# Order of PSUM reads and weight-chunk splits on VectorE and ScalarE in a two-layer hybrid attention trunk

## The reference

```
h = rms_norm(x); z = h @ w_in                 # columns cq, ckv, kr, gq, gk, gv, a, g
# A, latent attention: q = rms(cq) @ w_uq, k and v = rms(ckv) @ w_ukv, norms, rope,
#    8 heads, block-causal softmax(q k^T) v
# B, gated linear attention, 4 heads, chunks of 64 tokens:
#    la = log_sigmoid(z_a @ w_gate + b)/16; suffix sums and decays = exp(...)
#    state = state * decay + (k * exp(..))^T v;  o = q @ state;  rms_norm(o) * silu(z_g)
x = x + concat(rms(A), B) @ w_out
h = rms_norm(x); u = causal_dwconv(h @ w_up); x = x + (silu(gate) * up) @ w_down
```

## Time and the profile before

| | |
|---|---|
| median of 3 runs | 2252.37 us (2251.55 to 2254.59) |
| the profiled execution, its own time | 2252.84 us |
| its span, first to last instruction | 2251.1 us |
| TensorE busy | 2171.3 us (96%) |
| VectorE busy | 1511.8 us (67%) |
| ScalarE busy | 1006.6 us (45%) |
| mean granted TensorE clock | 0.989 |

### The profile page before, as it was taken

The page is one execution under the profiler, slowest core; times in us unless marked ns, Lnnn a source line. Parts: engine busy times, 40 slices in busy tenths (PEclk is TensorE's granted clock), DMA queues, the critical chain, the costliest instruction groups (busy, mean ns, idle before and its releaser), DMA issues. The chain is left out here.

```text
span 2251.1 us, 26696 instructions
## 1 busy us (share of the span) xinstructions
PE 2171.3 (96%) x11132; PEld 1834.0 (81%) x11132; DVE 1511.8 (67%) x1804; ACT 1006.6 (45%) x1151; POOL 15.9 (1%) x18
## 2 busy tenths in 40 slices
PE   7799889999999999999997998899999999999999
PEld 6687768888888888888885876688888888888887
DVE  5554455787777777777754554568777777787676
ACT  5555544444334344444454554354344334444442
POOL 0010000000000000000000100000000000000000
PEclk9999999999999999999998999999999999999999
DMA  7544335565555555555553444355655555555553
GB/s 214 177 137 135 131 112 187 170 204 172 189 191 192 194 187 186 189 189 190 192 173 117 156 142 140 114 188 169 206 187 176 190 191 191 189 189 184 194 190 139
DMA packets 293708, 391.90 MB, mean 174 GB/s; under 512 B 10944, under 2 KB 200180, under 8 KB 293588
## 3 DMA queue, kind: packets, MB, share of 16 engines
q1 hardware_dynamic: 293332, 390.00, 52.4%
q0 software_dynamic: 256, 0.20, 0.1%
HBM read 388.07 MB, written 2.10 MB: 173 GB/s over the span
## 5 line engine op out<-in xcount | busy, mean ns | idle before, releaser
L828 DVE TENSOR_TENSOR lo<-raw,hi 128x2048 fp32r<-128x2048 f32 (+2 forms) x372 | 841.2, 2262 | 416.0 <-ACT hi L514 414.6
L514 ACT ACTIVATE hi<-raw 128x2048 fp32r<-128x2048 f32 (+2 forms) x372 | 704.0, 1893 | 657.8 <-PE G L1309 351.4
L1366 PE MATMUL G<-hx,hi 128*128 128x512 f32 x1408 | 497.4, 398 | 0.0
L1366 PE MATMUL X<-hx,hi 128*128 128x512 f32 x1408 | 496.7, 397 | 0.0
L1367 PE MATMUL X<-hx,lo 128*128 128x256 f32 x1408 | 395.2, 281 | 0.0
L1367 PE MATMUL G<-hx,lo 128*128 128x256 f32 x1408 | 395.2, 281 | 0.0
L1366 PEld LDWEIGHTS X<-hx,hi 128*128 128x128 f32 x1408 | 264.3, 188 | 64.6
L1366 PEld LDWEIGHTS G<-hx,hi 128*128 128x128 f32 x1408 | 264.4, 188 | 64.3
L1367 PEld LDWEIGHTS G<-hx,lo 128*128 128x128 f32 x1408 | 266.0, 189 | 0.8
L1367 PEld LDWEIGHTS X<-hx,lo 128*128 128x128 f32 x1408 | 266.0, 189 | 0.0
L1307 PE MATMUL G<-hi,hx 128*128 128x512 f32 (+1 forms) x512 | 203.0, 397 | 15.7 <-DVE gv L1098 11.0
(11 more groups left out here) (250 smaller groups left out, 2230.1 us busy)
## 6 DMA issues: line engine op xcount, KB each, us to landing
raw<-in_w_up SPq DMA_DIRECT2D x176, 1024.0 KB, 5.1
raw<-in_w_down SPq DMA_DIRECT2D x88, 1024.0 KB, 5.0
raw<-in_w_in SPq DMA_DIRECT2D x56, 1024.0 KB, 5.1
raw<-in_w_out SPq DMA_DIRECT2D x32, 1024.0 KB, 5.0
raw<-in_w_uq SPq DMA_DIRECT2D x8, 768.0 KB, 4.7
raw<-in_w_in SPq DMA_DIRECT2D x8, 640.0 KB, 4.1
raw<-in_w_ukv SPq DMA_DIRECT2D x4, 1024.0 KB, 5.1
xk<-in_x SPq DMA_DIRECT2D x4, 512.0 KB, 10.9
```

What stands on the lines that cost most here:

```text
L514: act.activation(hi[:, k % SLOTS, 0:n], raw[:, k % SLOTS, 0:n], ACT.Copy).then_inc(hi_ready, 1)
L828: dve.tensor_tensor(lo[:, s, 0:n], raw[:, s, 0:n], hi[:, s, 0:n].bitcast(F32), ALU.subtract).then_inc(lo_ready, 1)
L1366: pe.matmul(bank, w_hi[:, at:at + P], hx[:, tile, :], start=tile == 0, stop=False)
```

## The change

The change alters no operation, no count and no shape. It moves operations against the splits in the lists of ScalarE and VectorE, alike in both layers; the lists of TensorE, GpSimd and SyncE stay as they are. VectorE: gk's `by_token` and `copy_kraw(0)` go from behind splits 14 and 15 to ahead of split 14, `copy_kraw(1)` ahead of split 15, the `la` step ahead of 16, gq's `by_token` ahead of 20, each `q_out` ahead of the next split, `copy_values` of odd heads ahead of splits 30, 32, 34 and 36, all `a_split` ahead of split 37, states 0 and 1 ahead of 39, `copy_o(0)` ahead of 40, states 2 and 3 ahead of 41, `gate_o(0)` and `copy_o(1)` ahead of 43, `gate_o(1)` ahead of 44. ScalarE: `copy_v(0)` ahead of split 15, `copy_v(1)` ahead of 16, the decays ahead of `k_square(1)`, `exps` ahead of `a_square`, `a_split` ahead of split 37 and of `silu(0)`, `o_square(0)` ahead of 41; `q_square(0)` and `q_square(1)` each go behind one more split.

```diff
 ScalarE
                 act.activation(la, la, ACT.Exp, scale=-1.0).then_inc(gate_soft.sem, 1)
+                copy_v(0)
                 split(l, 15)
                 act.activation(la, la, ACT.Ln, bias=ones[:, 0:1]).then_inc(gate_soft.sem, 1)
-                copy_v(0)
+                copy_v(1)
                 split(l, 16)
-                copy_v(1)
                 k_square(0)
                 split(l, 17)
-                k_square(1)
                 act.activation(la, X[:, 2:4, :], ACT.Exp, scale=1.0 / TAU).then_inc(gate_decay.sem, 1)
                 act.activation(decay, X[:, 0, 0:16], ACT.Exp, scale=1.0 / TAU).then_inc(gate_decay.sem, 1)
+                k_square(1)
                 split(l, 18)
...
+                split(l, 23)
                 q_square(0)
-                split(l, 23)
-                q_square(1)
...
                 split(l, 24)
+                q_square(1)
...
                     split(l, k + 2)
+                    exps(2 * p)
+                    exps(2 * p + 1)
                     if p >= 1:
                         a_square(2 * p - 1)
-                    exps(2 * p)
-                    exps(2 * p + 1)
...
                 a_square(HEADS - 1)
-                silu(0)
-                split(l, 37)
                 for h in range(HEADS):   # a_split, high part
...
+                split(l, 37)
+                silu(0)
                 split(l, 38)
...
                 silu(1)
+                o_square(0)
                 split(l, 41)
-                o_square(0)
 VectorE
-                split(l, 14)
                 by_token(U_GK, K_GK + 3, gk)
+                copy_kraw(0)
+                split(l, 14)
+                copy_kraw(1)
                 split(l, 15)
-                copy_kraw(0)
-                split(l, 16)
-                copy_kraw(1)
                 dve.scalar_tensor_tensor(la, X[:, 2:4, :], 0.0, la, ALU.min, ALU.subtract).then_inc(gate_log.sem, 1)
+                split(l, 16)
                 split(l, 17)
...
-                split(l, 20)
                 by_token(U_GQ, K_GQ + 3, gq, GDK ** -0.5)
+                split(l, 20)
+                q_out(0)
                 split(l, 21)
-                q_out(0)
                 q_rope(0)
+                q_out(1)
                 split(l, 22)
-                q_out(1)
                 q_rope(1)
+                q_out(2)
                 split(l, 23)
-                q_out(2)
+                q_out(3)
                 q_rope(2)
                 split(l, 24)
-                q_out(3)
                 q_rope(3)
...
-                    split(l, k + 2)
                     if p >= 1:
                         copy_values(2 * p - 1)
+                    split(l, k + 2)
...
+                copy_values(HEADS - 1)
                 split(l, 36)
-                copy_values(HEADS - 1)
-                split(l, 37)
                 for h in range(HEADS):   # a_split, low part
-                    if h == 6:
-                        split(l, 38)
...
+                split(l, 37)
+                split(l, 38)
...
-                split(l, 39)
                 state_step(0)
                 state_step(1)
+                split(l, 39)
+                copy_o(0)
                 split(l, 40)
-                copy_o(0)
+                state_step(2)
+                state_step(3)
                 split(l, 41)
                 add_to_x_when_done(l, U_OUT, a_rs)
                 split(l, 42)
-                state_step(2)
-                state_step(3)
                 gate_o(0)
+                copy_o(1)
                 split(l, 43)
                 add_to_x_when_done(l, U_OUT + 1, a_rs)
-                copy_o(1)
+                gate_o(1)
                 split(l, 44)
-                gate_o(1)
```

More of the change, by code:

```diff
@@ L652, in _, with copy_v @@
                 act.activation(la, la, ACT.Exp, scale=-1.0).then_inc(gate_soft.sem, 1)
+                def copy_v(j):
+                    act.wait_ge(slot_free, done(l, K_UKV + j))
+                    act.activation(v[:, :, 512 * j:512 * j + 512], bank2(U_UKV + 2 * j + 1), ACT.Copy).then_inc(v_copied.sem, 1)
+                copy_v(0)
                 split(l, 15)
@@ L655, in _ @@
                 act.activation(la, la, ACT.Ln, bias=ones[:, 0:1]).then_inc(gate_soft.sem, 1)
-                def copy_v(j):
-                    act.wait_ge(slot_free, done(l, K_UKV + j))
-                    act.activation(v[:, :, 512 * j:512 * j + 512], bank2(U_UKV + 2 * j + 1), ACT.Copy).then_inc(v_copied.sem, 1)
                 def k_square(j):
@@ L1090, in by_token @@
                     ins.then_inc(unit_free.sem, 1)
-                split(l, 14)
-                by_token(U_GK, K_GK + 3, gk)
                 def copy_kraw(j):
@@ L1098, in copy_kraw @@
                     dve.tensor_copy(kraw[:, :, 512 * j:512 * j + 512], bank2(U_UKV + 2 * j)).then_inc(unit_free.sem, 1)
+                by_token(U_GK, K_GK + 3, gk)
+                copy_kraw(0)
+                split(l, 14)
+                copy_kraw(1)
                 split(l, 15)
-                copy_kraw(0)
-                split(l, 16)
-                copy_kraw(1)
                 dve.wait_ge(gate_soft.sem, gate_soft.at(l, 3))
                 dve.scalar_tensor_tensor(la, X[:, 2:4, :], 0.0, la, ALU.min, ALU.subtract).then_inc(gate_log.sem, 1)
+                split(l, 16)
                 split(l, 17)
```

## The result

The changed kernel takes 2166.03 us (median of 4 runs, 2165.29 to 2166.48), against 2253.48 us for the kernel before beside it (4 runs, 2251.55 to 2254.91). The ratio is 0.9616, with a 95% interval of 0.9604 to 0.9627: 3.8% faster. Predicted were 2167 us in a range of 2161 to 2187.

The account below looks back on a forecast made before the run. TensorE was taken to bound the kernel. Waits 64.0, clock 17.9 and overlap 4.5 us sum to 86.4 us, taking 2252.84 us to 2166.4; the forecast was 2167 us, range 2161 to 2187.

Parts of the forecast that it names:

- What bounds the kernel: Whole kernel: TensorE, busy 2171.3 of 2251.1 us, sets the end; only its idle time, clock and matmul overlap count.
- The ten lines: TensorE's waits at steps the change moves, in both layers: 28 waits, 64.0 us in all.
- Step 1: TensorE's waits: walking the new order with old durations, none of the ten lines' waits is left, 64.0 us saved.
- four narrow places: Time in hand in the walk: copy_v(0) 1.6 us, copy_kraw(1) 1.4, q_out(2) 2.3, gate_o(1) 2.1.
- Steps 2 and 3: TensorE: full clock returns behind long waits, 17.9 us; matmul overlap lost at 28 waits returns, 4.5 us.
- Step 4: ScalarE's own moves (k_square(1), q_square, silu(0)) cost nothing; at most 1 us a layer if keys come late.
- Step 5: SyncE's loads, issued later behind a late lo, cost nothing; bounds 0 and 1 us for each late load.
- A: Rival: the narrow places come back as short waits, about 2 us at each of eight, 2183 us; chance 0.12.
- B: Rival: TensorE's idle time goes but the clock stays as it was, 2184 us; chance 0.04.
- C: Rival: loads become the bound, ten a layer each late by 1 us, 2187 us; chance 0.03.
- E: Rival: nothing changes, since the waits have another last releaser than the one named, 2252 us; chance 0.01.
- D: Rival: VectorE's reads ahead of subtractions make lo late and TensorE wait for it, slower, 2314 us; chance 0.02.

Follow-up runs that it names:

- e6: Changed kernel plus two reductions of constants on VectorE between the wait for the second key half and its copy, copy_kraw(1): 2165.90 us.
- e7: Changed kernel plus six reductions of constants on VectorE between the wait for the second key half and its copy, copy_kraw(1): 2171.70 us.
- three stage kernels: Kernel before with the new order in one stretch only: split 14 to the attention loop 2209.64 us, attention loop 2240.35, from split 37 on 2219.60.
- e4: Kernel before with the new order only in the attention loop, up to split 36, on both engines: 2240.35 us, ratio 0.9954.
- e5: Kernel before with the new order only from split 37 on, on both engines: 2219.60 us, ratio 0.9859.
- e11: Kernel before with VectorE's new list, and on ScalarE only copy_v(0) moved ahead of split 15 and the Ln: 2165.07 us, ratio 0.9613.
- e2: Kernel before with the new order on ScalarE alone, VectorE as before: 2243.07 us, ratio 0.9953.
- e9: Changed kernel plus ten reductions on VectorE between copy_kraw(0) and the subtraction of chunk 14: 2173.21 us.

## Why the prediction was right

Point by point, by its own steps. **What bounds the kernel**: the reading held. The ten lines were the whole of what could be had, and VectorE and ScalarE, with 30% and more of idle time, did not become the bound. **Step 1, idle time**: 64.0 us forecast, 63.9 measured. The walk through the new order with the old durations gave the margins to 0.1 us at all four narrow places, and e6 and e7 bracket the narrowest. The wide ones hold as well: `a_split` ends 8.0 us before it is wanted (1305.56 against 1313.59; the walk 8), the first two states 4.9 us (1319.03 against 1323.94; the walk 5), the others 7.6 us (1337.84 against 1345.48; the walk 7). That the waits are each their own is shown by the three stage kernels. **Steps 2 and 3, clock and overlap**: 17.9 + 4.5 = 22.4 us forecast, 23.2 measured as the fall in busy time. The sum held because every long wait went, and with them every stretch at a lower granted clock; for a part of the change the same reading was off by 4 us, as e4 and e5 show. Had the change removed only some of the waits, a forecast as near as this one would have been luck. **Step 4, ScalarE's other moves at nothing**: right for the whole change (e11), but for a reason that the step did not give: `q_square`'s move frees `q_out(2)` by itself (e2), and VectorE's move frees it again. The gain could be had twice and is counted once. **Step 5, loads**: ScalarE waits for loads of `w_in` three times, 4.5 us in all, as it did before the change (three times, 4.6 us), and e9, with the load of chunk 17 some 6 us later still, has no more (4.2 us).

**The rivals.** A did not come: the narrow places held in both layers. B fell: the clock is 1.00 over the mixer. C and E fell with the waits. D, the slower case, is a real mechanism, and its price was half right. VectorE does go in order, and a late subtraction does reach TensorE (e9), but through the next PSUM read in VectorE's list rather than through `lo`. The step that was mis-sized is "4.1 us late stands against a further 4.8 us before TensorE asks": what was in hand is 3.4 us, because I took TensorE's next wish for chunk 14 and not the copy that VectorE must do between. The 7.3 us in that step is also added up wrongly: it leaves out the 4.1 us by which the walk's `lo` is late already, so by its own numbers it is 4.1 + 4.8 + 2.5 = 11.4 us, and with the measured 3.4 it is 10.0. Neither slip mattered for the result.

## What to carry to other kernels

When an engine that does not set the end is idle a third of the time and the engine that does still waits for it, look at what stands ahead of the awaited operation in its list: here each was prefetch work, two chunks ahead of need, which was itself waiting. Put reads that free a bank ahead of prefetch, and then walk the new order through with measured durations, following every list to the next operation that TensorE asks for and not only to the delayed one. Price the clock behind waits as a whole, since of two waits of the same length and place one can cost it and the other not.

## What the runs showed of the hardware

The same wait of TensorE, 2.16 us before the same chunk, was followed by a granted clock of 0.66 in layer 0 and 1.00 in layer 1 (e7, means over 5 us); a wait of 2.42 us at the same place in e9 by 1.00 in layer 0 and 0.66 in layer 1; waits of 2.46 us by 0.66 in both layers of the kernel before and 1.00 in both of e4. With these waits the runs of one kernel spread widely (the kernel before from 2249.2 to 2258.1 us over all its runs), and without them little (the changed kernel from 2165.3 to 2166.5 us in four runs). That the spread comes from the clock was not separately tested.
